# A hybrid mixer and mixture-of-experts block: routing in tiles, with the counts first, the router ahead of the shared gate-up, and a last accumulation signalled bank by bank

## What is computed

```
h = rms_norm(x) * (1 + scale2) + shift2
scores = sigmoid(h @ w_router)                        # 64 experts, 8 groups of 8
biased = scores + router_bias
keep the 4 groups with the largest sum of their two best biased scores
choose the 8 best biased experts of those groups
w = scores of the chosen / their sum * 2.5
routed = sum over chosen e of w_e * (silu(h @ Wg_e) * (h @ Wu_e)) @ Wd_e
shared = (silu(h @ Sg) * (h @ Su)) @ Sd
x = x + gate2 * (routed + shared)
```

## Time and profile before

| | us |
|---|---|
| median of three runs | 758.88 (756.77 to 760.61) |
| profiled execution | 758.44 |
| its span in the trace | 756.6 |
| TensorE busy | 683.3 (90%) |
| VectorE busy | 307.8 (41%) |
| ScalarE busy | 167.9 (22%) |
| POOL busy | 28.5 (4%) |
| mean granted TensorE clock | 0.966 |

### The profile page before, as it was taken

The page is one execution under the profiler, slowest core; times in us unless marked ns, Lnnn a source line. Parts: engine busy times, 40 slices in busy tenths (PEclk is TensorE's granted clock), DMA queues, the critical chain, the costliest instruction groups (busy, mean ns, idle before and its releaser), DMA issues.

```text
span 756.6 us, 10005 instructions
## 1 busy us (share of the span) xinstructions
PE 683.3 (90%) x3369; PEld 385.7 (51%) x3369; DVE 307.8 (41%) x700; ACT 167.9 (22%) x291; POOL 28.5 (4%) x49
## 2 busy tenths in 40 slices
PE   2799999899999999798999979989999998899894
PEld 0478856677788467464344333433433343343342
DVE  2247987665724256652322221231222222212214
ACT  2010142111341113022222211221222122122221
POOL 7001111000000000000000000000000000000000
PEclk9789999999999999899999989999999999999997
DMA  8998989323331000484699999999999999999951
GB/s 307 387 378 288 389 310 344 120 109 112 112 139 56 0 1 3 162 339 167 247 427 428 424 424 430 422 426 429 428 423 427 426 429 424 424 430 427 423 234 56
DMA packets 43133, 225.66 MB, mean 298 GB/s; under 512 B 3488, under 2 KB 3520, under 8 KB 29414
## 3 DMA queue, kind: packets, MB, share of 16 engines
q1 hardware_dynamic: 41528, 224.43, 73.6%
q10 hardware_dynamic: 1582, 0.94, 0.5%
HBM read 224.31 MB, written 1.05 MB: 298 GB/s over the span
## 4 chain that ended last, share of the span: by engine, by line
PE 58%; DMA 30%; DVE 5%; SPq 2%; issue 2%; ACT 1%; ACTq 1%; DVEq 0%
DMA raw<-n_w_experts_gate_up_dram 27%; PE bank L1119 13%; PE bank L1415 13%; PE bank L1364 4%; PE bank L1399 4%; PE bank L1239 4%; PE bank L1271 4%; DMA ring<-in_w_ada_dram 3%; PE bank L1405 2%; PE bank L1147 2%; PE bank L1423 1%; PE bank L1375 1%; DVE work L748 1%; SPq L323 1%; SPq L319 1%
## 5 line engine op out<-in xcount | busy, mean ns | idle before, releaser
L1119 PE MATMUL bank<-work,ring 128*128 128x256 f32 x512 | 118.0, 388 | 1.4 <-ACT work L482 1.4
L1415 PE MATMUL bank<-raw,hT 128*32 128x512 f32 x832 | 99.8, 635 | 18.4 <-DMA raw<-n_w_experts_gate_up_dram 18.4
L1119 PEld LDWEIGHTS bank<-work,ring 128*128 128x128 f32 x512 | 98.4, 195 | 17.1 <-issue 2.6
L1399 PE MATMUL bank<-raw,hT 128*128 128x512 f32 x224 | 99.9, 599 | 2.8 <-ACT hT L593 2.8
L1019 DVE TENSOR_TENSOR sg<-sg,bank 128x256 f32<-128x256 f32 x27 | 11.4, 421 | 170.2 <-ACT sg L602 170.2
L1415 PEld LDWEIGHTS bank<-raw,hT 128*32 128x32 f32 x832 | 31.5, 116 | 85.4 <-issue 85.4
L1375 PE MATMUL bank<-y,ST 128*128 128x512 f32 x224 | 70.7, 438 | 2.3 <-DVE y L1028 2.3
L1399 PEld LDWEIGHTS bank<-raw,hT 128*128 128x128 f32 x224 | 41.4, 190 | 61.0 <-issue 58.5
L1405 PE MATMUL bank<-raw,aT 128*128 128x512 f32 x112 | 51.7, 604 | 7.4 <-ACT aT L607 7.4
L611 ACT ACTIVATE y<-bank,wcol 128x512 fp32r<-128x512 f32 x54 | 34.2, 684 | 108.5 <-PE bank L1405 54.3
L602 ACT ACTIVATE sg<-bank 128x256 f32<-128x256 f32 x27 | 17.2, 636 | 182.2 <-PE bank L1415 100.7
(11 more groups left out here) (289 smaller groups left out, 612.3 us busy)
## 6 DMA issues: line engine op xcount, KB each, us to landing
raw<-n_w_experts_gate_up_dram SPq DMA_DIRECT2D x53, 2048.0 KB, 16.7
raw<-in_w_experts_down_dram SPq DMA_DIRECT2D x53, 1024.0 KB, 18.4
ring<-in_w_ada_dram SPq DMA_DIRECT2D x12, 2048.0 KB, 18.4
ring<-in_w_in_dram SPq DMA_DIRECT2D x9, 2048.0 KB, 13.1
ring<-in_w_out_dram SPq DMA_DIRECT2D x2, 2048.0 KB, 7.8
ring<-in_w_attn_out_dram SPq DMA_DIRECT2D x1, 2048.0 KB, 18.9
ring<-in_w_conv_out_dram SPq DMA_DIRECT2D x1, 2048.0 KB, 7.9
ring<-in_w_shared_gate_up_dram SPq DMA_DIRECT2D x1, 2048.0 KB, 7.8
```

Of the source, the lines that this page charges most:

```text
L1119: ins = mm(b[:, kk * SEQ:(kk + 1) * SEQ], w[:, k, m * PART:(m + 1) * PART], h1T[:, k, :], start=(k == 0), stop=(k == KD - 1))
L1399: ins = mm(psU[:, :], hT[:, k, :], wg[:, k, :], start=(k == 0), stop=(k == KD - 1))
L1415: ins = mm(psU[c:c + 32, :], hT[:, k, c:c + 32], w_gu(s)[:, k, :], start=(k == 0), stop=(k == KD - 1))
```

## The change

- Buffers: the big expert goes to buffer 1, the mid one to 2, the small ones to 0 and 3. SP fetches the big expert after `tabs_ready` alone. The loop lengths have a signal of their own, `tally_ready`, and the waits for the shared pieces stand in front of the first small expert.
- h2 is written in two halves of its blocks, and its high and low parts are made tile by tile (`h2_hi`, `h2_lo`).
- The choice of experts is made tile by tile (`choose`), with the groups' four best found by MAX8 and MATCH_REPLACE instead of by pairs. `lower8` goes.
- TensorE does each tile's logits ahead of its shared gate-up. The gate-up's output blocks are put between the small matmuls of the routing. The counts come first of these (`cnt_done`), the ranks after.
- The tally moves from VectorE to three comparisons and eight operations on POOL, a matmul, and a copy on ScalarE.
- The first `select` uses banks 6 and 7. The shared down-projection moves as a whole into the gather, in front of its second quarter.
- The last scatter signals each of its four banks. VectorE multiplies all four, POOL adds the first two to x and VectorE the last two.

```diff
-        BIG, MID, SMALL = 0, 1, (2, 3)
+        BIG, MID, SMALL = 1, 2, (0, 3)
...
-            sp.wait_ge(*users[SHGU])
-            sp.wait_ge(*users[SHD])
             sp.wait_ge(tabs_ready, 1)
-            n_trio, n_big = loop_counts(sp)
             e = expert_of(sp, 0)
             load_gu(BIG, e)
             load_dn(BIG, e)
+            sp.wait_ge(tally_ready, 1)
+            n_trio, n_big = loop_counts(sp)
             for s in (MID,) + SMALL:
                 e = expert_of(sp, trio_rank(s, 0, n_big, n_trio))
+                if s == SMALL[0]:
+                    sp.wait_ge(*users[SHGU])
+                    sp.wait_ge(*users[SHD])
...
+            pool.wait_ge(left_ready, 1)
+            for i, least in enumerate((0.0, 64.0, 32.0)):
+                pool.tensor_scalar(tcol[:, i:i + 1], left, least, None, ALU.is_gt).then_inc(tcol_ready, 1)
+            pool.wait_ge(tally_in, 1)
+            link(pool.tensor_scalar(nb, many[:, 0:1], 0.25, -0.625, ALU.mult, ALU.add))
+            link(pool.tensor_scalar(nb, nb, WHOLE, -WHOLE, ALU.add, ALU.add))
+            pool.tensor_scalar(tab[0:1, 0:1], nb, 2.0, None, ALU.max)
+            link(pool.tensor_scalar(nb, nb, 2.0, None, ALU.max))
+            pool.tensor_scalar(na, nb, -3.0, many[:, 0:1], ALU.mult, ALU.add)
+            link(pool.tensor_scalar(other, nb, -1.0, many[:, 2:3], ALU.mult, ALU.add))
+            link(pool.tensor_scalar(na, na, many[:, 1:2], other, ALU.max, ALU.max))
+            pool.tensor_scalar(tab[0:1, 1:2], nb, 1.0, na, ALU.add, ALU.max).then_inc(tally_ready, 1)
...
+            for i in range(2):
+                pool.wait_ge(fin_gated, i + 1)
+                xo = xs[:, 0, i * W:(i + 1) * W]
+                pool.tensor_tensor(xo, xo, iota[:, i * W:(i + 1) * W], ALU.add).then_inc(fin_pool, 1)
...
+                if t == 0:
+                    h2_hi(0)
+                else:
+                    a.dma_start(rbias, router_bias.broadcast_to([PART, E])).then_inc(rb_in, 16)
+                    exp_z(0)
...
+            def choose(t):
+                v.wait_ge(ez_ready, t + 1)
+                link(v.tensor_scalar(r["e"][:, t], r["e"][:, t], 1.0, None, ALU.add))
+                link(v.reciprocal(r["s"][:, t], r["e"][:, t]))
+                if t == 0:
+                    v.wait_ge(rb_in, 16)
+                link(v.tensor_tensor(r["b"][:, t], r["s"][:, t], rbias, ALU.add))
                 for g in range(GROUPS):
+                    ins = v.max(top2[:, t, g, :], grp["b"][:, t, g, :])
+                link(ins)
+                link(v.tensor_tensor(gs[:, t], top2[:, t, :, 0], top2[:, t, :, 1], ALU.add))
+                link(v.max(gtop[:, t], gs[:, t]))
+                link(v.memset(gtop[:, t, TOPG:GROUPS], -NEG))
+                link(v.match_replace(grep[:, t], gtop[:, t], gs[:, t], -2.0 * NEG))
+                link(v.tensor_tensor(gout[:, t], grep[:, t], gs[:, t], ALU.is_equal))
+                link(v.scalar_tensor_tensor(grp["m"][:, t], gout[:, t].unsqueeze(2).broadcast_to([PART, GROUPS, EPG]), NEG,
+                                            grp["b"][:, t], ALU.mult, ALU.add))
+                link(v.max(top8[:, t, :], r["m"][:, t, :]))
+                link(v.match_replace(r["rep"][:, t, :], top8[:, t, :], r["m"][:, t, :], 2.0 * NEG))
+                v.tensor_tensor(r["sel"][:, t], r["rep"][:, t], r["m"][:, t], ALU.not_equal).then_inc(sel_out, 1)
...
+            h2_turned(0)
+            router_logits(0)
+            wsh = arrived(SHGU)
+            pe.wait_ge(x1_ready, 2)
+            shared_up(0, 0)
+            shared_up(0, 1, range(0, 4))
+            h2_turned(1)
+            shared_up(0, 1, range(4, KD))
+            pe.wait_ge(x1_ready, 4)
+            router_logits(1)
+            shared_up(1, 0)
...
+            shared_up(1, 1).then_inc(sgu_done, 1)
+            shared_up(0, 2, range(0, 4))
+            pe.wait_ge(sel_out, 2)
...
+            ins.then_inc(ecum_done, 1)
+            shared_up(0, 2, range(4, KD))
+            pe.wait_ge(tcol_ready, 3)
+            mm(bank[6][0:1, 0:3], ones[:, 0:1], tcol, start=True, stop=True).then_inc(tally_ps, 1)
+            shared_up(0, 3, range(0, 4))
+            pe.wait_ge(tabs_ps_in, 1)
+            mm(bank[7][0:1, 0:CAND], startv, perm, start=True, stop=True)
+            mm(bank[7][0:1, CAND:2 * CAND], expc[:, :], perm, start=True, stop=True).then_inc(tabs_ps, 1)
+            shared_up(0, 3, range(4, KD))
             pe.wait_ge(slotT_out, 1)
...
+            shared_up(1, 2)
...
+            pe.wait_ge(tally_in, 1)
+            pe.wait_ge(tabs_ready, 1)
             select(0)
+            shared_up(1, 3).then_inc(sgu_done, 1)
             for q in range(4):
                 pe.wait_ge(SS_ready, 2 * q + 2)
                 if q == 0:
-                    pe.wait_ge(h2r_lo, 1)
+                    pe.wait_ge(h2r_lo, 2)
+                if q == 1:
+                    shared_down()
...
-            ins = scatter(PASSES, stop=True)
-            ins.then_inc(all_done, 1)
+            for i in range(2 * TH):
+                scatter(PASSES[2 * i:2 * i + 2], stop=True).then_inc(all_done, 1)
```

More of the change, by code:

```diff
@@ L156, in hybrid_conformer_fox_moe_block @@
         sq2 = view(work, 0, 2 * D, TH)
[L157 to L158 removed]
+        shT = hT[:, 0:4, :].rearrange("p (m k) n -> p m (k n)", m=2)
+        shg = hT[:, 4:8, :].rearrange("p (m k) n -> p m (k n)", m=2)
         r = {n: work[:, 3072 + 128 * i:3200 + 128 * i].rearrange("p (t e) -> p t e", t=TH)
[L160 removed]
+             for i, n in enumerate(("z", "s", "b", "e", "m", "rep", "sel"))}
         rbias = work[:, 4096:4096 + E]
@@ L180, in hybrid_conformer_fox_moe_block @@
         left, keycol, rank, startv = (work[:, 5712 + i:5713 + i] for i in range(4))
[L181 to L184, removed]
+        tcol = work[:, 5720:5723]
+        many = work[0:1, 5724:5727]
+        nb, na, other = (work[0:1, 5728 + i:5729 + i] for i in range(3))
         Emat = split[0:E, IN_SPLIT:IN_SPLIT + SLOTS]
@@ L897, in _ @@
[L897 to L907, removed]
+                if t == 1:
+                    clip(0)
@@ L909, in _ @@
+            choose(0)
+            clip(1)
+            choose(1)
+            v.wait_ge(sel_out, 2)
             link(v.tensor_tensor(wt[:, :, :], r["s"], r["sel"], ALU.mult))
@@ L911, in _ @@
             link(v.reciprocal(st2[:, 0:2], st2[:, 0:2]))
[L912 to L925, removed]
-            link(v.scalar_tensor_tensor(slotm[:, :, :], slotm[:, :, :], 1.0, r["sel"], ALU.add, ALU.mult))
-            v.tensor_scalar(slotm[:, :, :], slotm[:, :, :], -1.0, None, ALU.add).then_inc(slotT_out, 1)
+            v.wait_ge(cnt_done, 1)
@@ L929, in _ @@
             v.tensor_copy(ecnt, bank[0][:, 448:449]).then_inc(ecol_out, 1)
-            v.wait_ge(ecol_out, 1)
-            v.tensor_scalar(counts[:, 0:E], cnt, float(PART), None, ALU.min)
-            link(v.tensor_scalar(counts[:, E:CAND], cnt, -float(PART), 0.0, ALU.add, ALU.max))
-            link(v.tensor_scalar(left, ecnt, offc[:, 0:1], 0.0, ALU.subtract, ALU.max))
+            v.tensor_scalar(left, bank[0][:, 448:449], offc[:, 0:1], 0.0, ALU.subtract, ALU.max).then_inc(left_ready, 1)
+            v.tensor_scalar(counts[:, 0:E], bank[0][:, 128:128 + E], float(PART), None, ALU.min)
@@ L934, in _ @@
+            link(v.tensor_scalar(counts[:, E:CAND], bank[0][:, 128:128 + E], -float(PART), 0.0, ALU.add, ALU.max))
             v.wait_ge(iota_ready, 1)
-            v.scalar_tensor_tensor(keyrow, counts, float(CAND), iota[:, 0:CAND], ALU.mult, ALU.subtract)
-            link(v.tensor_scalar(keycol, left, float(PART), float(CAND), ALU.min, ALU.mult))
-            link(v.tensor_tensor(keycol, keycol, pcol[:, :], ALU.subtract))
+            v.wait_ge(sel_ready, 1)
+            v.wait_ge(left_ready, 1)
@@ L938, in _ @@
+            v.scalar_tensor_tensor(keyrow, iota[:, 0:CAND], -1.0 / CAND, counts, ALU.mult, ALU.add)
+            link(v.tensor_scalar(keycol, left, float(PART), pcol[:, 0:1], ALU.min, ALU.subtract))
             link(v.tensor_scalar(above, keyrow, keycol, None, ALU.is_gt))
@@ L1304, in _ @@
+            shared_up(0, 2, range(0, 4))
+            pe.wait_ge(sel_out, 2)
+            for c in range(0, CAND, E):
+                for t in range(TH):
+                    mm(bank[0][c:c + E, 448:449], sel[:, t, :], ones[:, 0:1], start=(t == 0), stop=(t == TH - 1))
             for t in range(TH):
-                mm(bank[0][:, 128:128 + E], ones[:, :], sel[:, t, :], start=(t == 0), stop=(t == TH - 1))
+                ins = mm(bank[0][:, 128:128 + E], ones[:, :], sel[:, t, :], start=(t == 0), stop=(t == TH - 1))
@@ L1306, in _ @@
+            ins.then_inc(cnt_done, 1)
+            pe.wait_ge(z_ready, 2)
             for t in range(TH):
                 for s in range(t):
-                    mm(bank[0][:, 256 + t * E:256 + (t + 1) * E], ones[:, :], sel[:, s, :], start=(s == 0), stop=False)
```

(40 more changed lines are left out.)

186 lines of the change are left out of this document (85 added, 101 removed).

## The result

The changed kernel takes 749.38 us in the median of four runs (747.72 to 749.90), beside 757.89 for four of the kernel before: ratio 0.9873, 95% interval 0.9843 to 0.9903 (the ratios are those on record; the two medians alone give 0.9888). Forecast were 750.4 us and a gain of 8.5. The profiled execution, the fastest of the four at 747.72 us, has a span of 745.8 us (756.6 before) and a mean granted clock of 0.977 (0.966).

The account below looks back on a forecast made before the run. The end was taken to be set by the gather's end, plus a constant, plus the tail. Gains of 5.2 us at the gather's end and 3.3 in the tail, together 8.5, took 758.88 to 750.4 us; range 746.9 to 755.0.

Parts of the forecast that it names:

- The frame: Whole kernel: the end comes at the gather's end plus a constant plus the time of the last scatter and adds.
- idle DMA ahead of the gather's end: Between 340 and 349 us in the old profile the DMA engines move nothing; expected again before the fourth expert's fetch.
- the first fetch without worth: Fetching the first expert earlier (312.5 to 298) gains nothing by itself; the rival that it sets the end, 741, had 0.05.
- The constant: Expert loop from the fourth expert's fetch, at the gather's end, to the last scatter: fixed program, expected unchanged.
- The road to `sel`: Start to the completed choice of experts: `sel` 5.8 us earlier than at 296.7, with each `choose` taking 3.8.
- From `sel` to the gather: Routing between `sel` and the first gather matmul: 10.65 us plus 1.5 for a slow clock, instead of 17.1.
- the slow spell of 1.5 us: TensorE's small matmuls after `sel`: clock falls to 1.2 GHz again as in the old trace, adding 1.5 us.
- The gather: Gather: 33.95 us instead of 35.42, plus 6.93 of down-projection inside it, ending at 343.95 instead of 349.17.
- The uncovered down-projection: Shared down-projection inside the gather: 16 instructions on TensorE, 6.93 us, with nothing hiding them.
- The tail: Last scatter, final products and adds, last store: gain of 3.3 us; 2.0 if the engines' adds were fully serial.
- The late tally: Rival: `tally_ready` on POOL delays the gather's first copies; slower, 765 us at 3 us per operation; chance 0.05.
- The slow clock through the whole block: Rival: TensorE stays at 1.2 GHz for some 9 us of work after `sel`; gain only 4.0, 754.9 us; chance 0.10.

Follow-up runs that it names:

- the tail alone: Kernel before, given only the new ending (last scatter signals bank by bank, POOL adds the first two pieces): ratio 0.9950.
- the lump: Changed kernel with the shared gate-up blocks from between the routing's small matmuls put together behind the first `select`: 755.45 us, ratio 0.9934.
- the unaltered kernel in the second group of runs: Changed kernel with nothing altered, run again as yardstick for three edits beside it: 750.46 us, ratio 0.9885.
- the routing alone: Changed kernel with the ending (last scatter and final adds) of the kernel before: ratio 0.9907.

## Why the prediction was right, and where it was off

**The frame held**: idle DMA ahead of the gather's end, the first fetch without worth, the fourth fetch and then a constant. The constant was 396.0 and 395.9 us in the two first traces, and moving the first fetch by 14.4 us changed nothing. But it is less constant than the forecast had it: of the ten traces with these fetches four show 395.7 to 396.0 and six 397.3 to 400.9 (last section).

**The total** met the forecast closer than its parts did, and that is luck. The marks of the two traces give 10.0 us net of the 0.4 that is no effect of the change, the medians 8.5 (757.89 to 749.38), as forecast. The road and the clock came out 2.2 better than forecast and the tail 0.8 worse; the first expert, which the forecast had at nothing, costs 1.4 to 3 us in most executions traced with the new routing, but not in the one behind the marks. The interval of the ratio takes in both 8.5 and 10.

**The road to `sel`** was a little long. h2 was written by 281.68 (forecast 282.65, of which 0.4 is the execution's own shift); one `choose` took 3.82 and 3.83 from its first operation to `sel` (forecast 3.8), so most of the difference lies ahead of it. Gain 6.6 net of that shift instead of 5.8.

**From `sel` to the gather** I counted 10.65 at full clock, and every trace in which that stretch is unaltered shows 10.81 or 10.82. The step that failed is the slow spell of 1.5 us that I carried over from the earlier trace rows. It never came: the clock was 1.00 in every stretch from 286 to 304 us, and the spell came back when the blocks were taken out from between the small matmuls. The sentence of the Trainium skill weighed there (TensorE: Matmul & The Clock Gate, HAM oscillation: slow spells belong to starved stretches) agrees with both, and its sum for this stretch was the right one. The row of before had come from a different neighbourhood of matmuls, and I took the row without the neighbourhood.

**The gather**: 40.9 forecast, 41.0 measured to the fourth fetch. The uncovered down-projection was 6.87 for 6.93.

**The tail**: 3.3 forecast. Of seven traces with this tail three gave 3.3 (5.06, 5.06, 5.12) and four gave 2.5 (5.91 to 5.93). When POOL's pair took 2.50 us, VectorE's add beside it took 1.4 to 1.8; when it took 2.96 to 3.04, the adds took 0.69 and 1.04. The single adds show that the one that is first runs at its own speed and the other ends behind it. Here is the changed kernel, and under it the tail alone:

```profile
740.20 1.26 POOL L461 TENSOR_TENSOR xs<-xs,iota 128x512 f32<-128x512 f32 x1
...
740.41 1.59 DVE L1064 TENSOR_TENSOR xs<-xs,iota 128x512 f32<-128x512 f32 x1
```

```profile
745.58 0.69 DVE L1058 TENSOR_TENSOR xs<-xs,iota 128x512 f32<-128x512 f32 x1
745.67 1.72 POOL L448 TENSOR_TENSOR xs<-xs,iota 128x512 f32<-128x512 f32 x1
```

In the four long tails VectorE's first add ended 0.55 us after POOL's second, whether it had started 0.40, 0.21 or 0.12 us later than that or at the same time; in the three short ones POOL's ended 1.12 us after VectorE's. Where both started within 0.01 us of each other, it went one way in one trace and the other way in another. The long tails are those in which the last scatter took 2.87 to 3.27 us (granted clock 0.60 to 0.69 in it) instead of 2.11 to 2.86 (0.70 to 1.00), so that VectorE's third product came later; no run sets that clock, so this last link is argued. The tail's term was mis-sized in those cases: the forecast's 3.3 had the adds of the two engines pass freely. The Trainium skill (GPSIMD Engine Reference, Key points) names this contention. The traces agree: it costs 0.8 to 0.9 us between the two cases. With products beside POOL's adds only the edge of VectorE's first add is left of it (0.68 to 1.23 us in four traces).

**The rivals.** The late tally falls: 2.6 us for eight operations (293.05 to 295.65), as forecast, with 6 us to spare. The slow clock through the whole block falls for this kernel and is what the lump shows.

## What to carry to other kernels

Find the one event from which the rest of the program is fixed, and cost everything as a shift of that event; transfers that land before it can move either way without effect, as the first fetch did here. Count small matmuls between waits as a risk to the clock, and put independent large ones between them rather than ahead of them or behind. When two engines share an elementwise tail, let one of them do the operations that read a PSUM bank while the other does those with two SBUF operands; here that took the worst case away (5.9 to 5.3) and left the best where it was.

## Not expected: a slow first expert

The forecast's constant has a hole that only the further traces show. Between the gather's end and the first expert's gate-up TensorE pauses 2.8 us. In six of ten traces with that pause the clock was at 0.50 afterwards; in the kernel before, the tail alone, the changed kernel's first trace and the one with the tally on VectorE it was not. Stretches of the unaltered kernel in the second group of runs:

```profile
342.20:344.20 2.00, 1.99 (x3) 0.97 (x4) 0.86 (x3) 0.00 (x0) 0.00 (x0) 0.50 0.96 410
344.20:346.20 2.00, 2.00 (x5) 0.83 (x4) 0.00 (x0) 0.00 (x0) 0.00 (x0) 0.79 0.96 414
346.20:348.20 2.00, 2.00 (x6) 0.95 (x5) 0.00 (x0) 0.00 (x0) 0.00 (x0) 1.00 0.96 393
```

And of the kernel with the routing alone:

```profile
343.20:345.20 2.00, 2.00 (x3) 0.96 (x4) 0.83 (x3) 0.00 (x0) 0.00 (x0) 0.50 0.98 418
345.20:347.20 2.00, 2.00 (x4) 0.85 (x3) 0.00 (x0) 0.00 (x0) 0.00 (x0) 0.50 0.96 410
347.20:349.20 2.00, 2.00 (x3) 0.67 (x2) 0.00 (x0) 0.00 (x0) 0.00 (x0) 0.50 0.99 406
349.20:351.20 2.00, 2.00 (x6) 0.92 (x5) 0.00 (x0) 0.00 (x0) 0.00 (x0) 0.96 0.30 127
```

The first expert then reaches the first trio after 15.6 to 15.8 us (four traces) or 17.2 (two) instead of 14.0 to 14.2: 1.4 to 3 us. None of the four traces in which down-projection fills the pause has it. The loss arrives at the end, since from the first trio to the last scatter these traces take 378.9 to 381.1 us and the other four 378.9 to 379.4. All six are among the eight traces with the new routing and none among the two with the old; whether the change makes the spell more likely stays open. The fill may thus be worth more than the 2.9 us of the pause; four traces against ten are too few to say that it always prevents the spell, and what decides between one execution and the next with the same pause stays open.
